# Norm statistics computed with tokens on partitions, and normalised tiles handed over one at a time

## The chip, the cores and the metric

One core of one Trainium2 chip runs the whole program. The metric is the device time of one execution in microseconds (us): lower is better.

## The reference, cut to what matters

Two layers of a transformer-like backbone over 256 tokens (128 context, 128 latent), width 2048. Each layer normalises twice, and a last norm ends the program:

```python
def rms_norm(x, g):
    y = x * rsqrt(mean(x * x, axis=-1) + 1e-6)
    return y * g

for l in range(2):
    h = rms_norm(x, g_attn[l]) * (1 + scale1) + shift1     # norm1
    x = x + gate1 * (mixers(h @ w_in[l]) @ w_out[l])       # in1, in2, in3, attention, out
    h2 = rms_norm(x, g_mlp[l]) * (1 + scale2) + shift2     # norm2
    x = x + gate2 * (square(relu(h2 @ w_mlp1[l])) @ w_mlp2[l])   # up, down
y = rms_norm(x, g_final)
```

scale, shift and gate come from a product with w_ada (the "modulation"), one vector for the context tokens and one for the latent tokens. So there are five norms: q = 0 (layer 0, norm1), 1 (layer 0, norm2), 2, 3 (layer 1) and the final one.

## The kernel before

Everything is kept transposed: `xT[128, 16, 256]` holds feature 128k + p on partition p, the 16 feature tiles k, and 256 tokens (two groups s of 128) along the row. A weight matrix streams through in "pairs": 512 columns, loaded by SyncE as four 1 MB blocks `raw`; ScalarE rounds each half block to `hi`, VectorE takes the remainder `lo = raw - hi`, and TensorE multiplies both with the activations. The activations are split too: `hs[:, k, 0:256]` is the rounded part of tile k, `hs[:, k, 256:512]` its remainder. A pair is worked in two groups g of two output banks; a group has four steps h of four tiles k each, and step h needs the half block o = 4g + h of `hi` and `lo`. A tile k costs four matmuls: 128x512 (L447) and 128x256 (L449) for each of the two banks. Between the steps, TensorE also does eight-record units of the modulation product (L388).

The order on each engine is a Python walk over stages and pairs, the same on all engines; each engine runs its queue in order, and counting semaphores tie them together. A norm stage stands before the first `in1` pair and before the first `up` pair, and goes like this:

1. TensorE: one matmul of `ones` with `ssq` (L463; L586 for the final norm) sums the squares over the partitions, and leaves the sum on every partition: a 128x256 result in bank 7.
2. ScalarE: `std` = square root of that, 128x256 (L752; final L779).
3. VectorE: `rstd` = reciprocal of `std`, 128x256 (L1019; final L1055).
4. VectorE `ybuf` = x * amul * rstd (L1024), 128x128 for each tile and token group; ScalarE adds the shift and rounds into `hs` (L759); VectorE writes the remainder (L1032). In all 32 pieces of each kind, in a hardware loop of four rounds (`Fori`, UNROLL_K = 4 tiles a round): eight L1024, then eight L1032, then a wait for the last of them.

TensorE waits before each step h for `hs_ready` to show four more finished tiles. VectorE splits o = 0, 1, 2 of the pair ahead of the norm; the split of o = 3 (`lo`, L791), which step h = 3 needs, stands behind the norm in VectorE's queue. In the final norm, VectorE writes 32 pieces `yT` (L1058) from `rstd`; TensorE turns them back and they are stored.

```python
                    own.link(dve.reciprocal(rstd[:, :], std[:, :]))
                    with dve.Fori(0, KT // UNROLL_K) as i:
                        ...
                        dve.wait_ge(hs_ready, q * NORM_STEPS + S * UNROLL_K * (i + 1))
```

Of the kernel before, what the change touches and what calls it, by code (L numbers as in the profile page):

```python
# [53 lines left out]
UNROLL_K = 4  # L54
# [42 lines left out]
def build(nc, t):  # L97
# [28 lines left out]
    ones = place("ones", [P, P], f32)  # L126
    ssq = place("ssq", [P, TOK], f32)
    std = place("std", [P, TOK], f32)
    rstd = place("rstd", [P, TOK], f32)
    cT = place("cT", [P, KT, 32], f32)  # L130
    craw = place("craw", [P, S, KT], f32)
# [53 lines left out]
    def sem(name):  # L185
        return nc.alloc_semaphore(name)
# [15 lines left out]
    relu2_ready, hid_hi = sem("relu2_ready"), sem("hid_hi")  # L202
    x_updated, sq_ready, ssq_steps = sem("x_updated"), sem("sq_ready"), sem("ssq_steps")
    stat_ready, std_ready = sem("stat_ready"), sem("std_ready")
    ada_used, rows_ready = sem("ada_used"), sem("rows_ready")
    modps_ready, mods_done = sem("modps_ready"), sem("mods_done")
    dve_step = sem("dve_step")
# [96 lines left out]
    with block:  # L304
# [71 lines left out]

        @block.tensor
        def _(pe):
            def ada_unit(l, m, a, k):

                if k == 0:
                    pe.wait_ge(rows_ready, l * VECTORS + m)
                pe.wait_ge(ada_landed[k % 2], 16 * (2 * (a - PRE_JOBS) + (k % 4) // 2 + 1))
                ada_products(k, ada[:, k % 2])
# [46 lines left out]
            for l in range(DEPTH):  # L431
                def pair(kind, n, i, c, a, last, l=l):
                    acts = act2 if kind in ("out", "down") else hs
                    for g in range(2):

                        after(pe, bank_freed, 4 * n + 2 * g - 2)
                        for h in range(4):
                            pe.wait_ge(lo_ready, 8 * n + 4 * g + h + 1)
                            if kind == "down":
                                pe.wait_ge(act2_ready, hidden_base(l, c) + 4 * (h + 1))  # L440
                            elif kind != "out":
                                pe.wait_ge(hs_ready, (2 * l + (kind == "up")) * NORM_STEPS + 8 * (h + 1))
# [140 lines left out]


            pe.wait_ge(ssq_steps, ssq_base(DEPTH, -1))
            pe.matmul(pb[7][:, 0:TOK], ones[:, :], ssq[:, :], start=True, stop=True).then_inc(stat_ready, 1)  # L586
            for b in range(8):
                s, q = b % 2, b // 2
                pe.wait_ge(yT_ready, 8 * (q + 1))
# [7 lines left out]
        def _(act):  # L597
# [33 lines left out]
            for l in range(DEPTH):  # L631
# [117 lines left out]

                def norm(q, shift, l=l):  # L750
                    act.wait_ge(stat_ready, q + 1)
                    act.activation(std[:, :], pb[7][:, 0:TOK], ACT.Sqrt, bias=eps[:, :], scale=1.0 / D)\  # L752
                       .then_inc(std_ready, 1)
                    act.wait_ge(mods_done, vectors_done(l, shift))
                    with act.Fori(0, KT // UNROLL_K) as i:
                        for k in range(UNROLL_K):
                            for s in range(S):
                                act.wait_ge(norm_y, q * NORM_STEPS + S * UNROLL_K * i + 2 * k + s + 1)
                                act.activation(hs[:, bass.ds(UNROLL_K * i + k, 1), s * P:(s + 1) * P],  # L759
                                               ybuf[:, 2 * k + s:2 * k + s + 1, :], ACT.Identity,  # L760
                                               bias=mods[:, l, bass.ds(shift + UNROLL_K * i + k, 1), s])\
                                   .then_inc(norm_hi, 1)

                def stage(name, c, l=l):
                    if name == "norm1":
# [10 lines left out]
                walk(act, l, pair, stage)  # L776

            act.wait_ge(stat_ready, 2 * DEPTH + 1)
            act.activation(std[:, :], pb[7][:, 0:TOK], ACT.Sqrt, bias=eps[:, :], scale=1.0 / D).then_inc(std_ready, 1)  # L779
# [7 lines left out]
        def _(dve):  # L787
# [38 lines left out]
            for l in range(DEPTH):  # L826
# [185 lines left out]
                def norm(q, shift, scale, gain, l=l):  # L1012
# [3 lines left out]
                        amul[:, :, :], mods[:, l, scale:scale + KT, :], 1.0,  # L1016
                        vecs[:, l, 0, gain:gain + KT].unsqueeze(2).to_broadcast([P, KT, S]), ALU.add, ALU.mult))
                    dve.wait_ge(std_ready, q + 1)
                    own.link(dve.reciprocal(rstd[:, :], std[:, :]))  # L1019
                    with dve.Fori(0, KT // UNROLL_K) as i:  # L1020
                        for k in range(UNROLL_K):
                            for s in range(S):
                                tile = bass.ds(UNROLL_K * i + k, 1)
                                dve.scalar_tensor_tensor(  # L1024
                                    ybuf[:, 2 * k + s:2 * k + s + 1, :], xT[:, tile, s * P:(s + 1) * P],
                                    amul[:, tile, s], rstd[:, s * P:(s + 1) * P].unsqueeze(1),
                                    ALU.mult, ALU.mult).then_inc(norm_y, 1)
                        for k in range(UNROLL_K):
                            for s in range(S):
                                tile = bass.ds(UNROLL_K * i + k, 1)  # L1030
                                dve.wait_ge(norm_hi, q * NORM_STEPS + S * UNROLL_K * i + 2 * k + s + 1)
                                dve.scalar_tensor_tensor(  # L1032
                                    hs[:, tile, TOK + s * P:TOK + (s + 1) * P], ybuf[:, 2 * k + s:2 * k + s + 1, :],
                                    mods[:, l, bass.ds(shift + UNROLL_K * i + k, 1), s],
                                    hs[:, tile, s * P:(s + 1) * P].bitcast(f32),
                                    ALU.add, ALU.subtract).then_inc(hs_ready, 1)
# [15 lines left out]


            dve.wait_ge(std_ready, 2 * DEPTH + 1)
            own.link(dve.reciprocal(rstd[:, :], std[:, :]))  # L1055
# [73 lines left out]
```

## Time and profile before

| what | value |
|---|---|
| median of three runs | 2477.9 us (2466.62 to 2479.76) |
| the profiled execution | 2477.66 us, span 2475.9 us |
| granted TensorE clock, mean | 0.970 |
| TensorE busy | 2307.8 us, 93% of the span |
| VectorE busy | 1535.0 us, 62% |
| ScalarE busy | 1060.9 us, 43% |
| DMA | 570.29 MB, mean 230 GB/s |

The span is from the first to the last instruction; 1.8 us of the execution lie outside it. PE in a row is TensorE's matmuls, PEld its weight loads, DVE is VectorE, ACT is ScalarE, POOL is GpSimd, and a "q" behind an engine is its sequencer. L447 is line 447 of the kernel. PEclk is the granted TensorE clock, 1.00 for 2.4 GHz and 0.50 for 1.2 GHz. A matmul on fp32 operands leaves two records; those of L447 and L449, on the split (fp32r) operands, and transposes leave one.

### The profile page before, as it was taken

To read this page: it belongs to the slowest core of one execution; us is meant where nothing else is said; L and a number is where in the kernel's file an instruction comes from. 1 tells how busy PE (TensorE), PEld (TensorE's weight loads), DVE (VectorE), ACT (ScalarE), POOL (GpSimd) and SP (SyncE) were. 2 spreads that over 40 slices of the span, in tenths; PEclk is the share of its full clock that TensorE was granted. 3 is DMA by queue.
4 is the path that set the end of the run, shared out by engine and by line. 5 is a ranking of instruction groups with operands and counts; after the bars stand their busy time and mean duration, and the time that the engine had idled before them with its cause. 6 is when DMAs were issued, how large, how long until landed. Compare 5 with 4: busy or idle time off the path is not lost.

```text
span 2475.9 us, 37816 instructions
## 1 busy us (share of the span) xinstructions
PE 2307.8 (93%) x13176; PEld 1811.7 (73%) x13176; DVE 1535.0 (62%) x2606; ACT 1060.9 (43%) x1663; POOL 101.6 (4%) x196
## 2 busy tenths in 40 slices
PE   5699879979999999999997998797999999999998
PEld 1277556757887887787785775586788888888886
DVE  0457785565665665565567578767556666666666
ACT  1243334444444444454454333444345444444443
POOL 2000000000000000000000000000000000000000
PEclk9699999989999999999998999998999999999999
DMA  9888655858678668758855885354865655655652
GB/s 387 334 311 297 232 180 208 313 206 306 207 231 305 230 203 308 267 180 295 303 170 184 297 318 208 116 177 149 314 215 181 192 182 180 193 181 192 185 189 85
DMA packets 390555, 570.29 MB, mean 230 GB/s; under 512 B 9604, under 2 KB 364472, under 8 KB 365624
## 3 DMA queue, kind: packets, MB, share of 16 engines
q1 hardware_dynamic: 360504, 365.51, 44.8%
q0 software_dynamic: 27648, 201.34, 21.5%
q10 hardware_dynamic: 2304, 2.10, 0.2%
q8 instruction: 65, 1.06, 0.2%
q14 instruction: 34, 0.28, 0.0%
HBM read 565.76 MB, written 3.15 MB: 230 GB/s over the span
## 4 chain that ended last, share of the span: by engine, by line
PE 85%; DVE 6%; DMA 4%; ACT 2%; issue 1%; DVEq 1%; POOL 0%; ACTq 0%; POOLq 0%
PE bank L447 52%; PE bank L449 26%; PE bank L388 6%; DMA ada<-in_w_ada 4%; DVE qrs L921 1%; DVE yconv L884 1%; PE bank L463 1%; DVE lo L791 1%; DVE ybuf L1024 1%; DVE hs L1032 0%; DVEq L1032 0%; ACT hs L759 0%; ACT prob L739 0%; DVE yT L1058 0%; PE bank L406 0%
## 5 line engine op out<-in xcount | busy, mean ns | idle before, releaser
L447 PE MATMUL bank<-hs,hi 128*128 128x512 f32 x2944 | 1073.8, 407 | 47.9 <-DVE hs L1032 37.2
L791 DVE TENSOR_TENSOR lo<-raw,hi 128x1024 fp32r<-128x1024 f32 x685 | 817.5, 1223 | 479.0 <-ACT hi L602 477.5
L602 ACT ACTIVATE hi<-raw 128x1024 fp32r<-128x1024 f32 x685 | 706.4, 1053 | 583.8 <-PE bank L449 580.2
L447 PE MATMUL bank<-act,hi 128*128 128x512 f32 x2560 | 910.1, 400 | 5.4 <-DVE act L972 5.4
L449 PE MATMUL bank<-hs,lo 128*128 128x256 f32 x2944 | 829.7, 282 | 0.0
L447 PEld LDWEIGHTS bank<-hs,hi 128*128 128x128 f32 x2944 | 559.7, 190 | 298.4 <-issue 143.0
L449 PE MATMUL bank<-act,lo 128*128 128x256 f32 x2560 | 720.5, 281 | 0.0
L447 PEld LDWEIGHTS bank<-act,hi 128*128 128x128 f32 x2560 | 483.1, 189 | 137.2 <-issue 13.4
L449 PEld LDWEIGHTS bank<-hs,lo 128*128 128x128 f32 x2944 | 562.2, 191 | 2.5 <-issue 2.5
L449 PEld LDWEIGHTS bank<-act,lo 128*128 128x128 f32 x2560 | 485.8, 190 | 0.0
L647 ACT ACTIVATE tmp<-bank 128x256 f32<-128x256 f32 x344 | 113.5, 382 | 394.3 <-PE bank L449 394.3
L846 DVE TENSOR_TENSOR tsum<-bank,tmp 128x256 f32<-128x256 f32 x288 | 121.4, 421 | 201.0 <-ACT tmp L647 201.0
L388 PE MATMUL bank<-ada,cT 128*32 128x512 f32 x1344 | 185.7, 626 | 8.7 <-DMA ada<-in_w_ada 8.7
L364 POOL DMA_DIRECT2D ada<-in_w_ada x160 | 84.4, 528 | 1647.6 <-PE bank L388 1631.9
L658 ACT ACTIVATE thid<-xT 128x256 f32 (+1 forms) x160 | 66.8, 418 | 156.8 <-DVE xT L855 156.8
L855 DVE SCALAR_TENSOR_TENSOR xT<-tsum,mods,xT 128x128 f32 (+1 forms) x320 | 98.3, 349 | 36.8 <-DVE tsum L846 35.6
L884 DVE SCALAR_TENSOR_TENSOR yconv<-hpad,vecs,yconv 128x256 f32<-128x256 f32 x240 | 96.7, 482 | 0.0
L871 DVE TENSOR_TENSOR ssq<-ssq,thid 128x256 f32<-128x256 f32 x160 | 67.7, 423 | 27.9 <-ACT thid L658 25.5
L652 ACT ACTIVATE act<-thid 128x256 fp32r<-128x256 f32 x128 | 53.5, 418 | 67.2 <-DVE thid L849 67.2
L388 PEld LDWEIGHTS bank<-ada,cT 128*32 128x32 f32 x1344 | 26.9, 110 | 62.1 <-issue 39.0
L863 DVE TENSOR_TENSOR act<-thid,act 128x256 fp32r<-128x256 f32 x128 | 54.0, 422 | 9.6 <-ACT act L652 3.3
L759 ACT ACTIVATE hs<-ybuf,mods 128x128 f32 x128 | 39.6, 389 | 45.5 <-DVE ybuf L1024 45.3
(127 smaller groups left out, 714.3 us busy)
## 6 DMA issues: line engine op xcount, KB each, us to landing
raw<-in_w_mlp SPq DMA_DIRECT2D x256, 1024.0 KB, 6.2
ada<-in_w_ada POOLq DMA_DIRECT2D x168, 1024.0 KB, 6.0
raw<-in_w_in SPq DMA_DIRECT2D x56, 1024.0 KB, 6.2
raw<-in_w_out SPq DMA_DIRECT2D x32, 1024.0 KB, 5.7
pre_a<-in_w_ada POOLq DMA_DIRECT2D x16, 1024.0 KB, 18.4
pre_q<-in_w_ada POOLq DMA_DIRECT2D x8, 1024.0 KB, 18.6
xtok<-in_x_prompt SPq DMA_DIRECT2D x1, 1024.0 KB, 14.2
xtok<-in_x_sample SPq DMA_DIRECT2D x1, 1024.0 KB, 32.4
```

Of the source, the lines that this page charges most:

```text
L364: pool.dma_start(ada[:, k % 2, :], src[:, k, bass.ds(m * D, D)]).then_inc(ada_landed[k % 2], 16)
L388: mm = pe.matmul(ada_ps[32 * q:32 * q + 32, :], cT[:, k, :], unit[:, q * 512:(q + 1) * 512], start=(k == 0), stop=(k == KT - 1))
L447: pe.matmul(bank[:, :], hi[:, h, k, j * P:(j + 1) * P], acts[:, k_, :], start=(k_ == 0), stop=False)
L449: mm = pe.matmul(bank[:, TOK:2 * TOK], lo[:, h, k, j * P:(j + 1) * P], acts[:, k_, 0:TOK], start=False, stop=(k_ == KT - 1))
L602: act.activation(hi[:, o % 4, :, :], raw[:, (o // 2) % 4, 4 * (o % 2):4 * (o % 2) + 4, :], ACT.Copy).then_inc(hi_ready, 1)
L647: act.activation(tmp[:, j, :], pb[2 * g + j][:, TOK:2 * TOK], ACT.Copy)\
L658: act.activation(thid[:, j:j + 1, :], xT[:, bass.ds(4 * i + 2 * g + j, 1), :], ACT.Square).then_inc(sq_ready, 1)
L791: dve.tensor_tensor(lo[:, o % 4, :, :], raw[:, (o // 2) % 4, 4 * (o % 2):4 * (o % 2) + 4, :], hi[:, o % 4, :, :].bitcast(f32), ALU.subtrac ...
L846: dve.tensor_tensor(tsum[:, j, :], bank, tmp[:, j, :], ALU.add).then_inc(bank_freed, 1)
L855: dve.scalar_tensor_tensor(x, tsum[:, j:j + 1, s * P:(s + 1) * P], mods[:, l, bass.ds(gate + 4 * i + 2 * g + j, 1), s], x, ALU.mult, ALU.a ...
L871: dve.tensor_tensor(ssq[:, :], ssq[:, :], thid[:, j, :], ALU.add)\
L884: dve.scalar_tensor_tensor(y, hpad[:, ch, :, bass.ds(tap, P)], vecs[:, l, 1, bass.ds(4 * tap + ch, 1)], y, ALU.mult, ALU.add).then_inc(con ...
```

## The change

The sums of squares are computed with the tokens on partitions: for each token group s a matmul with `ssq` as the weights and one column of ones gives a 128x1 result. Square root and reciprocal then work on 128x2. Two matmuls, with that column broadcast along the row as the weights and the identity as the moving operand, spread the reciprocals back over all partitions into the other half of bank 7; VectorE reads them from there instead of from `rstd`. The loop of four rounds becomes straight code in which tile k + 2 is scaled before tile k is finished, and in the first group of the first pair after a norm TensorE waits for each tile. The statistics of attention's convolution still use `std` and `rstd`.

```diff
+            def norm_stats(q):
+                for s in range(S):
+                    mm = pe.matmul(pb[7][:, s:s + 1], ssq[:, s * P:(s + 1) * P], ones[:, 0:1], start=True, stop=True)
+                mm.then_inc(stat_ready, 1)
+                pe.wait_ge(tok_rstd_ready, q + 1)
+                for s in range(S):
+                    mm = pe.matmul(pb[7][:, TOK + s * P:TOK + (s + 1) * P],
+                                   tok_rstd[:, s:s + 1].to_broadcast([P, P]), ident, start=True, stop=True)
+                mm.then_inc(rstd_spread, 1)
...
+                        fresh = g == 0 and isinstance(i, int) and i == 0 and (
+                            kind == "in1" or kind == "up" and isinstance(c, int) and c == 0)
...
-                            elif kind != "out":
+                            elif kind != "out" and not fresh:
                                 pe.wait_ge(hs_ready, (2 * l + (kind == "up")) * NORM_STEPS + 8 * (h + 1))
                             for k in range(4):
+                                if fresh:
+                                    pe.wait_ge(hs_ready, (2 * l + (kind == "up")) * NORM_STEPS + 8 * h + 2 * (k + 1))
...
-                        column_sums(pb[7][:, 0:TOK], [ssq[:, :]]).then_inc(stat_ready, 1)
+                        norm_stats(2 * l + (name == "norm2"))
...
-                    act.activation(std[:, :], pb[7][:, 0:TOK], ACT.Sqrt, bias=eps[:, :], scale=1.0 / D)\
+                    act.activation(tok_std[:, :], pb[7][:, 0:S], ACT.Sqrt, bias=eps[:, :], scale=1.0 / D)\
                        .then_inc(std_ready, 1)
                     act.wait_ge(mods_done, vectors_done(l, shift))
-                    with act.Fori(0, KT // UNROLL_K) as i:
...
+                    for k in range(KT):
+                        for s in range(S):
+                            act.wait_ge(norm_y, q * NORM_STEPS + S * k + s + 1)
+                            act.activation(hs[:, k, s * P:(s + 1) * P], ybuf[:, 2 * (k % UNROLL_K) + s, :], ACT.Identity,
+                                           bias=mods[:, l, shift + k, s:s + 1]).then_inc(norm_hi, 1)
...
-                    own.link(dve.reciprocal(rstd[:, :], std[:, :]))
-                    with dve.Fori(0, KT // UNROLL_K) as i:
...
+                    dve.reciprocal(tok_rstd[:, :], tok_std[:, :]).then_inc(tok_rstd_ready, 1)
+                    dve.wait_ge(rstd_spread, q + 1)
+                    for step in range(KT + 2):
+                        if UNROLL_K <= step < KT:
+                            dve.wait_ge(hs_ready, q * NORM_STEPS + S * (step - UNROLL_K + 1))
+                        if step < KT:
                             for s in range(S):
                                 dve.scalar_tensor_tensor(
+                                    ybuf[:, 2 * (step % UNROLL_K) + s, :], xT[:, step, s * P:(s + 1) * P],
+                                    amul[:, step, s:s + 1], pb[7][:, TOK + s * P:TOK + (s + 1) * P],
                                     ALU.mult, ALU.mult).then_inc(norm_y, 1)
+                        k = step - 2
+                        if k >= 0:
                             for s in range(S):
+                                dve.wait_ge(norm_hi, q * NORM_STEPS + S * k + s + 1)
                                 dve.scalar_tensor_tensor(
+                                    hs[:, k, TOK + s * P:TOK + (s + 1) * P], ybuf[:, 2 * (k % UNROLL_K) + s, :],
+                                    mods[:, l, shift + k, s:s + 1], hs[:, k, s * P:(s + 1) * P].bitcast(f32),
                                     ALU.add, ALU.subtract).then_inc(hs_ready, 1)
-                        dve.wait_ge(hs_ready, q * NORM_STEPS + S * UNROLL_K * (i + 1))
...
-                                             vecs[:, 0, 2, V_GF + k:V_GF + k + 1], rstd[:, s * P:(s + 1) * P],
+                                             vecs[:, 0, 2, V_GF + k:V_GF + k + 1], pb[7][:, TOK + s * P:TOK + (s + 1) * P],
```

The final norm takes the same statistics, `norm_stats(2 * DEPTH)` on TensorE and the 128x2 square root and reciprocal.

## Rows read from the trace of the kernel before

**Rows 1.** The page's chain that ended last: shares of the span by line.

```profile
PE bank L447 52%; PE bank L449 26%; PE bank L388 6%; DMA ada<-in_w_ada 4%; DVE qrs L921 1%; DVE yconv L884 1%; PE bank L463 1%; DVE lo L791 1%; DVE ybuf L1024 1%; DVE hs L1032 0%; DVEq L1032 0%; ACT hs L759 0%; ACT prob L739 0%; DVE yT L1058 0%; PE bank L406 0%
```

**Rows 2.** Windows (A:B, length, busy of each engine, PEclk, DMA): norms, the MLP.

```profile
102.90:125.32 22.42, 13.54 (x64) 9.53 (x64) 19.63 (x66) 11.42 (x34) 0.94 (x2) 0.72 0.44 158
498.02:523.00 24.98, 14.35 (x66) 9.78 (x66) 20.84 (x67) 12.31 (x36) 1.05 (x2) 0.73 0.14 49
506.99:511.39 4.40, 4.40 (x13) 3.73 (x14) 3.91 (x14) 2.48 (x8) 0.00 (x0) 0.50 0.00 0
525.00:1100.00 575.00, 575.00 (x3327) 459.18 (x3326) 338.53 (x512) 255.61 (x370) 24.28 (x46) 1.00 0.73 253
1319.84:1344.21 24.37, 14.38 (x66) 9.83 (x66) 20.45 (x66) 12.30 (x36) 1.05 (x2) 0.72 0.13 44
1696.68:1720.88 24.20, 14.20 (x66) 9.69 (x66) 20.23 (x66) 12.06 (x35) 1.02 (x2) 0.74 0.13 44
2459.44:2462.47 3.03, 0.70 (x2) 0.30 (x2) 1.75 (x1) 0.47 (x1) 0.00 (x0) 0.66 0.00 0
```

**Rows 3.** Waits: engine and line, what it waited for, us, times, longest.

```profile
PE bank L447 <- DVE hs L1032: 37.2, 8, 9.6
```

**Rows 4.** Timeline of the norm q = 1: start, length, engine, line.

```profile
498.02 1.22 PE L463 MATMUL bank<-ssq,ones 128*128 128x256 f32 x2 [2.68 <-DVE ssq L871]
...
501.90 2.19 DVE L1024 SCALAR_TENSOR_TENSOR ybuf<-xT,amul,rstd 128x128 f32<-128x128 f32 x8 [0.35 <-DVE rstd L1019]
504.00 2.84 DVE L1032 SCALAR_TENSOR_TENSOR hs<-ybuf,mods,hs 128x128 f32 x8
506.99 0.77 PE L447 MATMUL bank<-hs,hi 128*128 128x512 f32 x1 [7.74 <-DVE hs L1032]
507.47 2.19 DVE L1024 SCALAR_TENSOR_TENSOR ybuf<-xT,amul,rstd 128x128 f32<-128x128 f32 x8 [0.63 <-DVE hs L1032]
523.00 4.63 DVE L791 TENSOR_TENSOR lo<-raw,hi 128x1024 fp32r<-128x1024 f32 x4 [0.21 <-DVE hs L1032]
```

**Rows 5.** Timeline: eight small matmul records and a modulation unit, at both clocks.

```profile
97.39 1.88 PE L406 MATMUL bank<-cst,rows 128*128 128x8 f32 x8 [0.72 <-ACT rows L608]
...
490.46 1.07 PE L388 MATMUL bank<-ada,cT 128*32 128x512 f32 x8
...
494.39 0.95 PE L406 MATMUL bank<-cst,rows 128*128 128x8 f32 x8
```

**Rows 6.** Groups by line and form: busy us, mean ns, idle before.

```profile
L602 ACT ACTIVATE hi<-raw 128x1024 fp32r<-128x1024 f32 x685 | 706.4, 1053 | 583.8 <-PE bank L449 580.2 <-issue 0.7
...
L1001 DVE RECIPROCAL rinv<-rsum 128x2 f32<-128x2 f32 x24 | 3.9, 164 | 1.7 <-ACT prob L739 1.2
...
L742 ACT ACTIVATE esink<-nb,sinks 128x2 f32<-128x2 f32 x12 | 3.5, 290 | 0.0
```

**Rows 7.** Timeline in attention: one 128x128 product (two records) at both clocks.

```profile
348.18 0.63 PE L566 MATMUL bank<-probT,vtok 128*128 128x128 f32 x2
...
354.43 0.39 PE L544 MATMUL bank<-kcT,zq 128*128 128x128 f32 x2
```

**Rows 8.** Timeline of the final norm: 32 pieces in straight code.

```profile
2462.47 8.49 DVE L1058 SCALAR_TENSOR_TENSOR yT<-xT,vecs,rstd 128x128 f32<-128x128 f32 x32
```

**Rows 9.** VectorE's sequencer at L1032: count, min/median/max ns.

```profile
L1032 DVEq FUSED_REGOPS  x224: 65/93/99, 106.6 to 1720.2; - x112
```

**Rows 10.** Groups: VectorE with a PSUM operand, without one, without and with a pointer operand.

```profile
L846 DVE TENSOR_TENSOR tsum<-bank,tmp 128x256 f32<-128x256 f32 x288 | 121.4, 421 | 201.0 <-ACT tmp L647 201.0
L884 DVE SCALAR_TENSOR_TENSOR yconv<-hpad,vecs,yconv 128x256 f32<-128x256 f32 x240 | 96.7, 482 | 0.0
...
L871 DVE TENSOR_TENSOR ssq<-ssq,thid 128x256 f32<-128x256 f32 x160 | 67.7, 423 | 27.9 <-ACT thid L658 25.5
L849 DVE SCALAR_TENSOR_TENSOR thid<-tsum 128x256 f32<-128x256 f32 x128 | 54.5, 425 | 4.4
```

**Rows 11.** A window in attention, TensorE alone: length, busy, PEclk, DMA.

```profile
366.00:368.00 2.00, 1.09 (x8) 1.00 0.05 21
```

More of the change, by code:

```diff
@@ L128, in build @@
     std = place("std", [P, TOK], f32)
+    tok_std = place("tok_std", [P, S], f32)
+    tok_rstd = place("tok_rstd", [P, S], f32)
     rstd = place("rstd", [P, TOK], f32)
@@ L204, in build @@
     stat_ready, std_ready = sem("stat_ready"), sem("std_ready")
+    tok_rstd_ready, rstd_spread = sem("tok_rstd_ready"), sem("rstd_spread")
     ada_used, rows_ready = sem("ada_used"), sem("rows_ready")
@@ L585, in _ @@
             pe.wait_ge(ssq_steps, ssq_base(DEPTH, -1))
-            pe.matmul(pb[7][:, 0:TOK], ones[:, :], ssq[:, :], start=True, stop=True).then_inc(stat_ready, 1)
+            norm_stats(2 * DEPTH)
             for b in range(8):
@@ L751, in norm @@
                     act.wait_ge(stat_ready, q + 1)
-                    act.activation(std[:, :], pb[7][:, 0:TOK], ACT.Sqrt, bias=eps[:, :], scale=1.0 / D)\
+                    act.activation(tok_std[:, :], pb[7][:, 0:S], ACT.Sqrt, bias=eps[:, :], scale=1.0 / D)\
                        .then_inc(std_ready, 1)
                     act.wait_ge(mods_done, vectors_done(l, shift))
-                    with act.Fori(0, KT // UNROLL_K) as i:
[L756 to L762, printed above, removed]
+                    for k in range(KT):
[3 more added lines that the diff above has]
+                                           bias=mods[:, l, shift + k, s:s + 1]).then_inc(norm_hi, 1)
                 def stage(name, c, l=l):
@@ L778, in _ @@
             act.wait_ge(stat_ready, 2 * DEPTH + 1)
-            act.activation(std[:, :], pb[7][:, 0:TOK], ACT.Sqrt, bias=eps[:, :], scale=1.0 / D).then_inc(std_ready, 1)
+            act.activation(tok_std[:, :], pb[7][:, 0:S], ACT.Sqrt, bias=eps[:, :], scale=1.0 / D).then_inc(std_ready, 1)
             for b in range(8):
@@ L1018, in norm @@
                     dve.wait_ge(std_ready, q + 1)
-                    own.link(dve.reciprocal(rstd[:, :], std[:, :]))
-                    with dve.Fori(0, KT // UNROLL_K) as i:
-                        for k in range(UNROLL_K):
+                    dve.reciprocal(tok_rstd[:, :], tok_std[:, :]).then_inc(tok_rstd_ready, 1)
[4 more added lines that the diff above has]
+                        if step < KT:
@@ L1022, in norm @@
                             for s in range(S):
-                                tile = bass.ds(UNROLL_K * i + k, 1)
                                 dve.scalar_tensor_tensor(
-                                    ybuf[:, 2 * k + s:2 * k + s + 1, :], xT[:, tile, s * P:(s + 1) * P],
-                                    amul[:, tile, s], rstd[:, s * P:(s + 1) * P].unsqueeze(1),
+                                    ybuf[:, 2 * (step % UNROLL_K) + s, :], xT[:, step, s * P:(s + 1) * P],
+                                    amul[:, step, s:s + 1], pb[7][:, TOK + s * P:TOK + (s + 1) * P],
@@ L1027, in norm @@
                                     ALU.mult, ALU.mult).then_inc(norm_y, 1)
-                        for k in range(UNROLL_K):
+                        k = step - 2
+                        if k >= 0:
                             for s in range(S):
-                                tile = bass.ds(UNROLL_K * i + k, 1)
-                                dve.wait_ge(norm_hi, q * NORM_STEPS + S * UNROLL_K * i + 2 * k + s + 1)
+                                dve.wait_ge(norm_hi, q * NORM_STEPS + S * k + s + 1)
@@ L1032, in norm @@
                                 dve.scalar_tensor_tensor(
-                                    hs[:, tile, TOK + s * P:TOK + (s + 1) * P], ybuf[:, 2 * k + s:2 * k + s + 1, :],
-                                    mods[:, l, bass.ds(shift + UNROLL_K * i + k, 1), s],
-                                    hs[:, tile, s * P:(s + 1) * P].bitcast(f32),
+                                    hs[:, k, TOK + s * P:TOK + (s + 1) * P], ybuf[:, 2 * (k % UNROLL_K) + s, :],
+                                    mods[:, l, shift + k, s:s + 1], hs[:, k, s * P:(s + 1) * P].bitcast(f32),
@@ L1054, in _ @@
             dve.wait_ge(std_ready, 2 * DEPTH + 1)
-            own.link(dve.reciprocal(rstd[:, :], std[:, :]))
+            dve.reciprocal(tok_rstd[:, :], tok_std[:, :]).then_inc(tok_rstd_ready, 1)
+            dve.wait_ge(rstd_spread, 2 * DEPTH + 1)
             for k in range(KT):
```

## The prediction

> **What bounds the kernel now.** I read the chain that ended last first: 78% of the span is the two matmul lines L447 and L449, and every line of the norm has 1% or less [rows 1]. In the MLP stretch TensorE is busy for all of 575.00 us at clock 1.00 [rows 2]. So only stretches in which TensorE stands still can give anything. The waits name the one that this change touches: L447 waited 37.2 us for L1032, in eight waits [rows 3], four at the starts of the norms q = 0 to 3 and four inside them. The windows, cut from the moment at which the norm's own chain can begin (in q = 0 the end of the splits ahead of the reciprocal, else the matmul of ones) to the start of the `lo` split for step h = 3, show 22.42, 24.98, 24.37 and 24.20 us, with TensorE busy 13.5 to 14.4 us of each; the final norm needs 3.03 us from matmul to first piece [rows 2].
>
> The timeline of q = 1 says what fills such a window [rows 4]. 498.02 to 501.90, 3.88 us: matmul of ones at the low clock (1.22), square root, reciprocal, start of the loop (0.35 idle). 501.90 to 523.00, 21.1 us: four rounds of eight L1024 in 2.19 us and eight L1032 in 2.84 us, with 0.63 us idle between rounds. TensorE starts at 506.99. But that start does not set the end of the stage: step h = 3 needs `lo` of o = 3, which begins behind the last L1032 at 523.00 and takes 1.2 us of the 4.63. VectorE's chain through the norm is the bound, and whatever shortens it moves the rest of the program, which is solid TensorE work, by as much. An earlier first matmul alone gives nothing.
>
> **The change, part by part.** *Statistics.* New: two one-column matmuls. The nearest rows are four products with eight columns in 0.95 us at the high clock and 1.88 us at the low one [rows 5], so 0.48 or 0.94 us for two. A ScalarE operation on 128x2 takes 0.29, a reciprocal on 128x2 0.16 [rows 6], where the 128x256 one took 1.75 (DVE busy in the window of the final norm [rows 2]). Spreading: two 128x128 products, each 0.63 us at the low clock and 0.39 at the high [rows 7], 1.26 or 0.78 us if they don't overlap (the lower bound is one of them, 0.39). Four hand-overs between engines: the final norm's 3.03 us hold 0.70, 0.47 and 1.75 us of work and so 0.11 us for three [rows 2], 0.04 each, 0.15 to 0.2 us. Sum: 0.94 + 0.29 + 0.16 + 1.26 + 0.2 = 2.8 us at the low clock; 2.4 us if the first pair still runs high, which I take for q = 2; 1.9 us for the final norm, all high. In q = 0 the statistics lie under VectorE's three splits already, and only reciprocal, spreading and hand-overs stay: 1.5 us. TensorE's new wait for the reciprocal delays nothing: behind it are only the matmuls that need the norm. No DMA is moved, and SyncE's and POOL's queues keep their order.
>
> *The tiles.* VectorE still issues 64 pieces of 128x128. In straight code 32 of them took 8.49 us [rows 8], which is (8.49 - 0.35) / 31 = 0.263 us from start to start. L1024 holds that pace in the loop, (2.19 - 0.35) / 7 = 0.263; L1032 takes up to (2.84 - 0.35) / 7 = 0.356 [rows 4], and its sequencer spent 224 register operations of 93 ns on 128 pieces [rows 9]. Straight code has constants there and none of the pauses between rounds. Bounds for one L1032: 0.263 and 0.356; I take 0.263, since the only thing the loop adds goes. Then piece 64 ends 63 x 0.263 + 0.35 = 16.9 us after the first starts. ScalarE, behind piece 58 (15.3 us), needs 0.4 for its last tile and 1.05 for `hi` of o = 3 [rows 6]: 16.8. So the `lo` split starts at 17.2, with 0.2 to 0.3 us of gap as before.
>
> *PSUM operand.* L1024 and L1058 now read bank 7. A 128x256 operation with a PSUM operand took 421 ns, one without 423; what does cost is a pointer operand, 482 against 425 [rows 10], and those pieces have it already. I take 0; the bounds are 0 and the 57 ns of that pair, 160 pieces x 0.057 = 9.1 us. The Trainium skill speaks against this edit: VectorE: DVE Perf Modes, section "The TRN2 errata", gives VectorE a fixed 58 cycles from SBUF and 120 from PSUM; as an estimate that is 65 ns x 160 = 10.3 us, so about 2469 instead of 2459. Both rows at 421 to 423 ns speak against it.
>
> *Hand-over by tile.* Tile k is whole after piece 4k + 8: tile 0 at 2.2 us, tile 11 at 51 x 0.263 + 0.35 = 13.8 us. A tile's four matmuls take 0.69 us at the high clock (575 us for 3327 records) and 0.63 x 2 = 1.26 at the low (seven pairs in 4.40 us [rows 2]). TensorE follows the tiles and is through with h = 2 and two modulation units of 1.07 us [rows 5] at about 13.8 + 0.7 + 1.3 = 15.8 us, before the first `lo` is there at 17.2 + 1.2 = 18.4. This edit is worth nothing by itself: what hides it is the wait for `lo`; without that cover it would be worth up to 2.6 us a stage.
>
> **The sum.** Stages after: 1.5 + 17.2 = 18.7; 2.8 + 17.2 = 20.0; 2.4 + 17.2 = 19.6; 20.0. Against [rows 2]: 3.7 + 5.0 + 4.8 + 4.2, and 3.0 - 1.9 = 1.1 for the final norm: 18.8 us. The profiled execution took 2477.66 us, within 0.3 of the median: 2477.7 - 18.8 = 2459 us, 0.76% faster.
>
> **Rivals.**
> *PSUM reads cost.* 57 ns on each of 160 pieces: 2468. For it, no row; against it [rows 10].
> *The pieces keep their pace.* If the 0.356 us of L1032 comes from its wait on ScalarE and not from the registers, 32 x 0.093 = 3.0 us a stage come back, 12 us: 2471. For it: L1032 is the line with a wait. Against: ScalarE is two tiles ahead now.
> *The low clock holds.* Handing over by tile leaves TensorE busy 0.69 of each 1.05 us, 66%, for 12 us. If the clock stayed at 1.2 GHz, twelve tiles take 15.1 us and two units 4.3: ready at 2.2 + 19.4 = 21.6, 3.2 later than `lo`, and step h = 3 costs 2.3 more: 5.5 x 4 = 22 us, 2481. Against it: in attention TensorE was busy 1.09 of 2.00 us at clock 1.00 [rows 11]. The Trainium skill (TensorE: Matmul & The Clock Gate, "A second HAM failure mode: psum-queue depth-cycling") has a kernel in which short idle times between groups made the clock swing; that is this rival.
> *Slower than before.* The same mechanism carried on: 18.8 + 12.4 = 31 us must be lost, so the low clock must also last through another step and a half of full TensorE work in every stage (2.3 us for each step): about 2492. Against it: in q = 1 TensorE, once fed, spent only 4.40 us at 0.50 [rows 2].
>
> **How the numbers follow.** A measurement here can tell about 0.5% from no change, 12.4 us: 2465.5 is the border. Forecast, 2450 to 2465, 0.70; below 2450 (the lowest run of before lay 11 us under its median) 0.06; PSUM 0.09; pace 0.07; low clock 0.05; slower 0.03. Range 2450 to 2470: it takes in the PSUM bound and, nearly, the pace rival; 0.80 or a little more lies inside. Faster: 0.70 + 0.06 + 0.02 of the PSUM case that falls short of its bound = 0.78; same 0.19; slower 0.03.
>
> **What the profile after would show.** Right: from first to last piece of a norm about 17 us, L1024 and L1032 interleaved at 0.263; small reciprocal 0.16 us; L447's first wait for L1032 shorter by about 4 us, and the wait for `lo` before h = 3 left at 2 to 3 us; the window up to that split 19 to 20 us; the MLP stretch unchanged. Wrong: pieces from bank 7 longer than 350 ns; PEclk 0.50 beyond the first 6 us of tiles; TensorE still at h = 2 when `lo` is there.

## The result, and the profile after

The changed kernel takes 2440.57 us (median of 4 runs, 2439.11 to 2461.4) where the kernel before, in the same session, takes 2477.69 (4 runs, 2466.62 to 2479.76): ratio 0.9876, 95% interval 0.9841 to 0.991. That is 37 us faster, twice the 18.8 us of the sum and below the range of 2450 to 2470. The profiled execution took 2439.11 us (span 2437.4), 38.55 us less than the profiled one before.

The chain of the page answers [rows 1]: the same two matmul lines (now L466 and L468), with the same shares.

```profile
PE bank L466 52%; PE bank L468 26%; PE bank L403 6%; DMA ada<-in_w_ada 4%; DVE hs L1050 1%; DVE ybuf L1042 1%; DVE qrs L937 1%; DVE yconv L900 1%; DVE lo L807 1%; PE bank L482 0%; ACT prob L758 0%; DVE yT L1075 0%; PE bank L421 0%; PE bank L390 0%; PE bank L510 0%
```

Windows of the changed kernel. Those of q = 1, q = 2, q = 3 and the final norm are cut at the same events as in [rows 2]. Then come TensorE's first tiles of q = 1 in two windows, from its first matmul at 500.49 to 505.00 and on to 509.40, and the MLP stretch.

```profile
495.35:514.86 19.51, 15.51 (x72) 11.21 (x72) 17.09 (x68) 12.18 (x35) 0.87 (x2) 0.75 0.18 61
1303.25:1322.35 19.10, 15.47 (x72) 11.01 (x72) 16.91 (x67) 12.18 (x35) 0.58 (x2) 0.73 0.17 56
1677.34:1696.85 19.51, 15.43 (x72) 10.84 (x72) 16.89 (x66) 12.18 (x35) 0.89 (x2) 0.77 0.15 54
2421.97:2424.12 2.15, 1.56 (x8) 1.18 (x8) 0.17 (x1) 0.26 (x1) 0.00 (x0) 0.85 0.00 0
500.49:505.00 4.51, 4.51 (x14) 3.83 (x15) 4.51 (x19) 2.97 (x9) 0.00 (x0) 0.50 0.00 0
505.00:509.40 4.40, 4.40 (x28) 2.97 (x27) 4.40 (x19) 3.01 (x10) 0.53 (x1) 0.98 0.18 32
525.00:1100.00 575.00, 575.00 (x3364) 462.04 (x3363) 341.09 (x515) 257.63 (x373) 23.77 (x45) 1.00 0.74 254
```

The four stages came out a little shorter than forecast: 19.51, 19.10 and 19.51 us against 20.0, 19.6 and 20.0; q = 0, from the reciprocal at 103.09 to the split at 121.24, 18.15 against 18.7. The final norm is a little longer than forecast, 2.15 us against 1.9. Against [rows 2] they give 4.27 + 5.47 + 5.27 + 4.69 + 0.88 = 20.6 us. Some 18 us of the 38.5 between the two spans are not in the norms.

The timeline of q = 1 (start, length, engine, line) shows the new chain: 2.83 us from 495.35 to 498.18, the first tile of TensorE 2.31 us after the first piece, and the last pieces running into the split of step h = 3.

```profile
495.35 1.01 PE L386 MATMUL bank<-ones,ssq 128*128 128x1 f32 x4 [2.68 <-DVE ssq L887]
496.41 0.26 ACT L771 ACTIVATE tok_std<-bank,eps 128x2 f32<-128x2 f32 x1 [1.56 <-PE bank L386]
496.70 0.17 DVE L1035 RECIPROCAL tok_rstd<-tok_std 128x2 f32<-128x2 f32 x1 [1.07 <-ACT tok_std L771]
496.92 1.22 PE L390 MATMUL bank<-cst,tok_rstd 128*128 128x128 f32 x4 [0.55 <-DVE tok_rstd L1035]
498.18 1.64 DVE L1042 SCALAR_TENSOR_TENSOR ybuf<-xT,amul,bank 128x128 f32<-128x128 f32 x6 [1.31 <-PE bank L390]
...
500.49 0.76 PE L466 MATMUL bank<-hs,hi 128*128 128x512 f32 x1 [2.35 <-DVE hs L1050]
...
513.28 1.66 DVE L1050 SCALAR_TENSOR_TENSOR hs<-ybuf,mods,hs 128x128 fp32r<-128x128 f32 x6
514.86 1.22 DVE L807 TENSOR_TENSOR lo<-raw,hi 128x1024 fp32r<-128x1024 f32 x1
```

The waits that answer [rows 3]: 37.2 us on the norm's tiles have become 9.4, and TensorE's new wait for the small reciprocal is 4.7. The wait for `lo` was there before and is nearly what it was, 10.7 and now 9.6 us. First a line of the kernel before, then three of the changed one:

```profile
PE bank L447 <- DVE lo L791: 10.7, 6, 2.6
```

```profile
PE bank L466 <- DVE lo L807: 9.6, 6, 2.3
PE bank L466 <- DVE hs L1050: 9.4, 4, 2.4
PE bank L390 <- DVE tok_rstd L1035: 4.7, 4, 3.0
```

**Where the other 18 us are.** The group of L666 (`tmp`, the first read of each finished bank) gives the moments at which groups of matmuls end. Here it is for the MLP of layer 1, 57 groups with no modulation unit among them, of the kernel before (L647) and then of the changed one (L666); the last numbers are the first and the last start:

```profile
L647 ACT ACTIVATE tmp<-bank x114: 378/383/385, 1821.9 to 2456.3; 128x256 f32<-128x256 f32 x114
```

```profile
L666 ACT ACTIVATE tmp<-bank x114: 378/382/385, 1796.4 to 2418.8; 128x256 f32<-128x256 f32 x114
```

634.4 us against 622.4: 12.0 us less in a stretch in which nothing was edited. Both kernels show TensorE 100% busy at clock 1.00 there, so the windows cannot see it. The groups by form can. Line L447 or L466 in layer 0's first `down` stretch (640 to 700) and in layer 1's MLP (1900 to 2400), kernel before:

```profile
L447 PE MATMUL bank<-act,hi 128*128 128x512 f32 x171 | 60.5, 399 | 0.0
...
L447 PE MATMUL bank<-act,hi 128*128 128x512 f32 x649 | 229.5, 399 | 0.0
```

and the changed kernel:

```profile
L466 PE MATMUL bank<-act,hi 128*128 128x512 f32 x175 | 60.7, 394 | 0.0
...
L466 PE MATMUL bank<-act,hi 128*128 128x512 f32 x716 | 248.3, 394 | 0.0
```

A tile step, one 512-column and one 256-column product, starts every 0.3533 us in the one and every 0.3467 us in the other (means over the start times). I call these the long and the short pace. Layer 0's four `down` stretches of 264 steps come to 4 x 264 x 0.0067 = 7.0 us, layer 1's MLP of 1792 steps to 11.9: 18.9 us, which with the 20.6 of the stages makes up the 38.5 within a microsecond (layer 1's attention took 1.1 us more).

Both paces are in every profile. Through the stretches with modulation units they alternate: a burst of 16 steps at the short pace, a unit, a burst at the long one. Over the 14 profiles of this case the pace changed at 1923 of the 1986 units that stand between two bursts. In the kernels without extra units, a stretch without units keeps the pace of the last burst ahead of it to its end, up to 630 us later. Which pace that is therefore hangs on where the few exceptions fall. So what was to be tested was whether this pace is the change's doing.

### The profile page after: what moved, and what is told of

It is laid out like the page before. It is cut to its first block, busy times and chain, and to the rows that moved or that the text cites. A ratio compares the mean times of both kernels' runs of the same rounds, so it can differ in the third digit from the quotient of the medians.

```text
span 2437.4 us, 36896 instructions
## 1 busy us (share of the span) xinstructions
PE 2293.2 (94%) x13206; PEld 1808.6 (74%) x13206; DVE 1520.0 (62%) x2606; ACT 1060.4 (44%) x1663; POOL 101.6 (4%) x196
## 3 DMA queue, kind: packets, MB, share of 16 engines
q0 software_dynamic: 27648, 201.34, 21.9%
q8 instruction: 65, 1.06, 0.2%
HBM read 565.76 MB, written 3.15 MB: 233 GB/s over the span
## 4 chain that ended last, share of the span: by engine, by line
PE 86%; DVE 7%; DMA 4%; ACT 2%; issue 1%; POOL 0%; ACTq 0%; DVEq 0%; POOLq 0%
PE bank L466 52%; PE bank L468 26%; PE bank L403 6%; DMA ada<-in_w_ada 4%; DVE hs L1050 1%; DVE ybuf L1042 1%; DVE qrs L937 1%; DVE yconv L900 1%; DVE lo L807 1%; PE bank L482 0%; ACT prob L758 0%; DVE yT L1075 0%; PE bank L421 0%; PE bank L390 0%; PE bank L510 0%
## 5 line engine op out<-in xcount | busy, mean ns | idle before, releaser
L466 PE MATMUL bank<-hs,hi 128*128 128x512 f32 x2944 | 1068.4, 406 | 19.2 <-DVE lo L807 9.6
L466 PE MATMUL bank<-act,hi 128*128 128x512 f32 x2560 | 895.6, 396 | 5.4 <-DVE act L988 5.4
L468 PE MATMUL bank<-hs,lo 128*128 128x256 f32 x2944 | 826.6, 281 | 0.0
L466 PEld LDWEIGHTS bank<-hs,hi 128*128 128x128 f32 x2944 | 559.5, 190 | 265.9 <-issue 112.9
L468 PE MATMUL bank<-act,lo 128*128 128x256 f32 x2560 | 712.1, 278 | 0.0
L466 PEld LDWEIGHTS bank<-act,hi 128*128 128x128 f32 x2560 | 481.7, 188 | 129.9 <-issue 13.4
L468 PEld LDWEIGHTS bank<-hs,lo 128*128 128x128 f32 x2944 | 561.3, 191 | 2.5 <-issue 2.5
L468 PEld LDWEIGHTS bank<-act,lo 128*128 128x128 f32 x2560 | 483.1, 189 | 0.0
L666 ACT ACTIVATE tmp<-bank 128x256 f32<-128x256 f32 x344 | 113.3, 382 | 384.7 <-PE bank L468 384.7
L865 DVE SCALAR_TENSOR_TENSOR thid<-tsum 128x256 f32<-128x256 f32 x128 | 54.4, 425 | 4.4
## 6 DMA issues: line engine op xcount, KB each, us to landing
pre_a<-in_w_ada POOLq DMA_DIRECT2D x16, 1024.0 KB, 18.8
pre_q<-in_w_ada POOLq DMA_DIRECT2D x8, 1024.0 KB, 18.8
```

What stands on the lines that cost most here:

```text
L666: act.activation(tmp[:, j, :], pb[2 * g + j][:, TOK:2 * TOK], ACT.Copy)\
```

## The experiments

**The changed kernel once more** (no edit).

> The changed kernel once more, beside the kernel before. Two theories. Theory A: the change shortens the four norm stages and the final norm, by about 20 us in all; the other 18 us of the first comparison are a pace of TensorE in the groups of matmuls that hold no modulation unit, 11.09 us a group against 11.31, which is picked in each execution and can fall to either kernel. Then the times of each kernel lie in clusters: the changed one near 2440 and near 2461, the one before near 2478, near 2466 and, if both layers come out fast, near 2458. Theory B (rival): the new order of the norm fixes the fast pace: all runs of the changed kernel within 2 us of 2440, none near 2461, and the one before never below 2466.

2438.06, 2440.38, 2440.47, 2445.88, 2451.52, 2458.93: ratio 0.9869 (0.9837 to 0.9902). The profiled run, 2445.88 us, has every stage as above (2.83 and 2.41 us to the first piece, 16.67 and 16.68 from there to the split), the long pace in layer 0 and the short one in layer 1:

```profile
L466 PE MATMUL bank<-act,hi 128*128 128x512 f32 x171 | 60.5, 399 | 0.0
...
L466 PE MATMUL bank<-act,hi 128*128 128x512 f32 x696 | 241.4, 394 | 0.0
```

2445.88 - 2439.11 = 6.8 us, the 7.0 of layer 0's stretches. The pace is not fixed by the program: it differs between runs of one kernel, so theory B is out, and the gain is 37 us with some luck in it. The final norm depends on the granted clock: 2.07 us here, 2.15 in the first profile, and 2.83 in other profiles of the changed kernel.

**The statistics alone** (loop and waits of before, spread statistics). The cut shows the edit against the changed kernel.

```
                     dve.wait_ge(rstd_spread, q + 1)
-                    for step in range(KT + 2):
+                    with dve.Fori(0, KT // UNROLL_K) as i:
...
+                                    amul[:, tile, s], pb[7][:, TOK + s * P:TOK + (s + 1) * P].unsqueeze(1),
...
-                        fresh = g == 0 and isinstance(i, int) and i == 0 and (
+                        fresh = False
```

> Only the statistics are changed; the loop of four rounds, with its pauses and the waits for four tiles, is kept. By the terms of the prediction: from the matmul of the sums to the first scaled piece 2.8 us where it was 3.9, from there to the split of o = 3 unchanged at 20.3 to 21.1 us, in sum 5 us less than before: 2473 at the slow pace of TensorE, 2452 to 2455 at the fast one. Theory B, if the statistics are what sets the pace: all runs near 2453.

Median 2476.91 of ten (2459.73 to 2481.53), ratio 0.9986 (0.9963 to 1.0009). The way to the first piece is 3.15 us where it was 3.88 (q = 1), the rest of the stage stays at 20.3 to 21.1:

```profile
499.46:523.71 24.25, 15.54 (x72) 11.34 (x72) 19.21 (x68) 12.09 (x36) 1.06 (x2) 0.73 0.15 52
```

Up to 0.7 us a stage and 0.6 to 1.1 in the final norm, under 4 us in all, is less than this measurement can tell. The expectation had 5 us, with 2.8 us to the first piece: of the 3.15, 0.36 lie idle between the spreading and the first piece, as 0.35 did in the loop of before [rows 4], and only the straight code drops them.

**The straight code and the waits by tile alone** (statistics of before, so all operands in SBUF). The cut shows the edit against the kernel before.

```
                     own.link(dve.reciprocal(rstd[:, :], std[:, :]))
-                    with dve.Fori(0, KT // UNROLL_K) as i:
+                    for step in range(KT + 2):
...
+                                    amul[:, step, s:s + 1], rstd[:, s * P:(s + 1) * P],
...
+                                if fresh:
+                                    pe.wait_ge(hs_ready, (2 * l + (kind == "up")) * NORM_STEPS + 8 * h + 2 * (k + 1))
```

> Only the straight order of the tiles and TensorE's wait for each tile; square root and reciprocal stay on 128x256. By the terms of the prediction: 3.5 to 3.9 us to the first piece as before, then 17.2 us to the split of o = 3 instead of 20.3 to 21.1, in sum 14 us less: 2464 at the slow pace, 2443 at the fast one. Theory B, if the order of the tiles sets the pace: all runs near 2443.

2455.78 us (2444.25 to 2464.75), ratio 0.9915 (0.9886 to 0.9945). First piece to split: 16.82 us in all four stages, 20.3 to 21.1 before, so 3.5 to 4.3 us each. The window of q = 1, and the piece that reads SBUF here:

```profile
494.80:515.17 20.37, 14.45 (x66) 9.30 (x66) 18.80 (x67) 12.40 (x35) 0.90 (x2) 0.78 0.17 59
...
L1026 DVE SCALAR_TENSOR_TENSOR ybuf<-xT,amul,rstd 128x128 f32<-128x128 f32 x128 | 38.2, 344 | 0.1
L1034 DVE SCALAR_TENSOR_TENSOR hs<-ybuf,mods,hs 128x128 fp32r<-128x128 f32 x128 | 38.2, 343 | 0.0
```

The same lines of the changed kernel, in which `ybuf` (L1042) reads bank 7:

```profile
L1050 DVE SCALAR_TENSOR_TENSOR hs<-ybuf,mods,hs 128x128 fp32r<-128x128 f32 x128 | 38.4, 347 | 0.0
L1042 DVE SCALAR_TENSOR_TENSOR ybuf<-xT,amul,bank 128x128 f32<-128x128 f32 x128 | 37.9, 343 | 5.3 <-PE bank L390 5.3
```

344 ns from SBUF, 343 from PSUM, and 16.82 against 16.68 us from first piece to split: the PSUM operand costs nothing.

**The changed kernel without the waits by tile.**

```
- fresh = g == 0 and isinstance(i, int) and i == 0 and (...)
+ fresh = False
```

> The changed kernel without TensorE's wait for each tile: it waits for four tiles again. The split of o = 3 should still be what step h = 3 waits for, so the same time as the changed kernel at the same pace, within 1 us (2440 or 2461). Rival: the early start of TensorE is worth something, for instance by bringing its clock up sooner: 2 us or more slower than the changed kernel at the same pace.

2442.9 us (2438.42 to 2450.45), ratio 0.9866 (0.9834 to 0.9898), the same as with them. TensorE's first tile starts 5.44 us after the first piece instead of 2.31, and the wait for `lo` has moved to the tiles:

```profile
PE bank L465 <- DVE hs L1049: 21.9, 4, 5.5
...
PE bank L465 <- DVE lo L806: 0.7, 2, 0.3
```

So the cover was just used up. The first `tmp` behind the split of h = 3 comes 21.1 us after the first piece in q = 0 and q = 1, as with the waits by tile, but 21.6 and 21.9 us after it in q = 2 and q = 3.

**One extra modulation unit ahead of the first `down` stretch of each layer**, in the kernel before and in the changed one, to turn the pace over.

```
+ elif name == "clear" and isinstance(c, int) and c == 0:
+     for q in range(4):
+         pe.matmul(pb[6][32 * q:32 * q + 32, :], cT[:, 0, :], cst[:, 0:512], start=True, stop=True)
```

> The kernel before with four more 32x512 products of the modulation's shape, on constants, into an unused bank, once in each layer between the last up pair of the first chunk and its down pairs (added work, 1.2 us each; its result is not used). In six profiles the pace of the matmul steps changes between 0.3467 and 0.3533 us with every modulation unit, and a stretch without units keeps the pace of the last steps ahead of it. If each unit turns the pace over, the first down stretch here has the other pace than the steps before the extra unit, in both layers, and the times move with it: the kernel before, mostly slow in both layers (2478 to 2484), comes out mostly near 2461 to 2465. Rival: the pace of the long stretches hangs on something else (the code of the loop, the data): then down stays at 0.3533 and the time is 2480 to 2486.

> The changed kernel with the same extra units. If each unit turns the pace over: the changed kernel, mostly fast in both layers (2438 to 2441), now mostly 2459 to 2463, and its own gain over the kernel with the extra units and the old norm stays near 20 us at the same pace. Rival: the change itself makes the long stretches fast: 2441 to 2444.

Before with the unit: 2484.33 us, all twelve runs from 2483.73 to 2488.18, ratio 1.0037 (1.0022 to 1.0052). After with it: 2459.5, six runs from 2458.81 to 2462.61, ratio 0.9937 (0.9916 to 0.9958). The spread is gone, and both stand at the long pace in their profiles. For the changed kernel that was expected. For the kernel before 2461 to 2465 was, and the time came out where the rival had put it, though nothing here shows the rival's reasons, the code of the loop or the data. TensorE's timeline in the changed kernel with the unit shows the place: a burst at the short pace, the eight small records of L421 (they stand there without an extra unit too, and the pace stays the same across them), the unit (L602, 1.06 us), and L466 at the long pace behind it:

```profile
612.65 0.39 PE L466 MATMUL bank<-hs,hi 128*128 128x512 f32 x1
612.88 0.27 PE L468 MATMUL bank<-hs,lo 128*128 128x256 f32 x1
612.99 0.40 PE L466 MATMUL bank<-hs,hi 128*128 128x512 f32 x1
613.22 0.28 PE L468 MATMUL bank<-hs,lo 128*128 128x256 f32 x1
613.34 0.95 PE L421 MATMUL bank<-cst,rows 128*128 128x8 f32 x8
614.22 1.06 PE L602 MATMUL bank<-cst,cT 128*32 128x512 f32 x8
615.22 0.50 PE L466 MATMUL bank<-act,hi 128*128 128x512 f32 x1
...
615.68 0.39 PE L466 MATMUL bank<-act,hi 128*128 128x512 f32 x1
...
616.03 0.40 PE L466 MATMUL bank<-act,hi 128*128 128x512 f32 x1
```

This makes the comparison that the first pair of profiles does not allow, the change at one pace: 2484.33 - 2459.5 = 24.8 us. The two profiles (spans 2482.2 and 2458.6, 23.6 apart) account for it. Norm windows, from the same events: 22.40 + 24.97 + 24.83 + 23.69 + 3.56 = 99.45 us against 18.16 + 19.51 + 19.51 + 19.50 + 2.83 = 79.51, 19.9 less. From the split of h = 3 to the first `tmp` behind it: 23.28 us in the four stages against 17.63, 5.7 less. Layer 1's `out` stretch had the short pace in the one and the long one in the other, 1.7 us back. 19.9 + 5.7 - 1.7 = 23.9.

The 5.7 us are the clock. Windows from that split to `tmp`, the changed kernel in q = 0 and q = 1, then the same kernel with the unit in q = 0:

```profile
121.24:127.17 5.93, 4.65 (x17) 4.03 (x18) 4.63 (x5) 2.77 (x3) 0.19 (x1) 0.71 0.78 257
514.86:519.22 4.36, 3.08 (x17) 2.73 (x18) 4.36 (x5) 2.77 (x4) 0.18 (x1) 1.00 0.71 249
```

```profile
121.28:125.68 4.40, 3.13 (x17) 2.75 (x18) 4.40 (x5) 2.77 (x3) 0.17 (x1) 1.00 0.79 246
```

TensorE waits there for `lo`, and in some stages its granted clock falls from 1.00 (2.4 GHz) to the low level (1.2 GHz) once more, which costs 1.5 us. In the first pair of profiles both kernels paid this twice. It was 17 of 20 stages with the norm's loop of before (five profiles) and 7 of 20 in the changed kernel (its own two profiles and three with extra units). The straight code with the old statistics paid it in three stages of four, so the count is no plain property of the straight code. It goes with the wait: in these 44 stages TensorE stood still for 2.0 to 2.6 us ahead of the split's first product, and each fall began in that wait or up to 1.3 us behind it. In the 12 stages of the three profiles in which TensorE's waits for `lo` are at most 0.3 us (without the waits by tile, and the split taken into the norm, below) the clock never fell. Why it falls behind some of these waits and not behind others is open.

**The split of h = 3 taken into the norm**, the step that the windows point to: TensorE waits for `lo`, and VectorE has all it needs for it earlier. ScalarE's `hi` split of the same step goes ahead of its part of the norm.

```
                     for step in range(KT + 2):
+                        if step == 12:
+                            split_lo(l * PAIRS_LAYER + (IN1 + IN2 + IN3 + OUT if q % 2 else 0), 3)
```

> The changed kernel with the split of o = 3 moved: ScalarE rounds it ahead of its square root, VectorE takes the remainder in the middle of the tiles, at step 12, so that step h = 3 doesn't wait behind the norm. If that wait is the bound of the stage, as the prediction says, TensorE starts step h = 3 about 2 us sooner in each of the four norms: 8 us less at the same pace, 2430 to 2433 where both layers are fast and 2450 to 2453 where both are slow. Rival: TensorE is the bound itself by then, and the 1.2 us of the split delay the last tiles: within 2 us of the changed kernel at the same pace.

2444.78 us (2432.16 to 2452.68), ratio 0.9866 (0.9834 to 0.9897). Windows from the split to the first `tmp`, q = 0 and q = 1:

```profile
116.18:124.52 8.34, 7.04 (x39) 4.70 (x38) 8.34 (x24) 5.67 (x13) 0.53 (x1) 1.00 0.66 222
507.07:515.41 8.34, 7.36 (x42) 5.05 (x41) 8.34 (x24) 5.66 (x13) 0.53 (x1) 1.00 0.80 258
```

`tmp` now comes 11.46 + 8.34 = 19.8 us after the first piece in every stage, where it was 21.1 or, with the fall of the clock, 22.6; that fall is gone. Four stages give 5 to 11 us. The profiled run, 2444.1 us, had the long pace in layer 1's MLP; less 11.9 that is 2432.2, and two of the six runs stand there, 2432.16 and 2433.7, where the changed kernel's lowest is 2438.06. The medians cannot tell the two apart (2444.78 and 2443.18): the pace spreads them by more than the edit gives.

**The kernel before once more** (no edit), profiled once.

> The kernel before, for one more profile. Norm stages as in the first profile to 0.1 us (3.9, 3.4 and 3.9 us to the first piece, 20.3 to 21.1 from there to the split); the pace of the down stretches one of 0.3467 and 0.3533 us in each layer, constant through each layer's MLP. If the pace is picked once per stretch with even chances, fast in both layers would show in one of four.

2483.35 us, long pace in all three stretches and four falls of the clock. The ways to the first piece are 3.87, 3.86 and 3.35 us, where 3.9, 3.4 and 3.9 were expected. With the first profile: 2483.35 - 2477.66 = 5.7 us, against 1.7 (`out`) + 2 x 1.5 = 4.7 counted.

**Two extra units, and one in layer 1 alone**, to see whether a unit turns the pace over or sets it. Kernel before and changed kernel with two (the loop runs over `range(8)`), changed kernel with `and l == 1`, and the split-inside kernel with two.

> The kernel before, with two extra modulation units (eight matmuls 32x512, results unused) instead of one ahead of the first down stretch of each layer. Two units should cost about 2 x 1.1 x 2 = 4.4 us at most by themselves. Theory A (each unit turns the pace of the two-matmul step over, 0.3467 to 0.3533 us and back, and the pace ahead of the unit was the short one in every profile with one extra unit): with two units the down stretches of both layers run at 0.3467, about 18.7 us less than with one unit: 2484.3 - 18.7 + 2.2 = 2468 us, and steady within 3 us. Theory B (an extra unit there always leaves the long pace behind, whatever was before): 2484.3 + 2.2 = 2486.5, steady. Theory C (the steadiness with one unit was chance): times spread over 2465 to 2487 as those of the kernel before do.

> The changed kernel with the same two extra units. Theory A: 2459.5 - 18.7 + 2.2 = 2443 us, steady within 3 us, and 25 us below the kernel before with two units, as with one (24.8). Theory B: 2461.7, steady. Theory C: spread from 2442 to 2463.

> The changed kernel with one extra unit in layer 1 alone. If what the unit does is bound to its own place, the layer 1 MLP stretch runs at 0.3533 in every run (11.9 us more than the all-fast 2438.5, so none below 2450) and the layer 0 stretch at either pace, as in the changed kernel: values near 2451.5 and near 2458.5. If the extra unit acts on the whole program (by where the instructions lie), layer 0 is slow in every run too: all near 2458.5.

> The changed kernel with the split of step h = 3 taken into the norm, and two extra units. Theory A: the all-fast value of that kernel, about 2432, + 4.4 for the two pairs of units = 2436 us, steady. Theory B: 2432 + 20.6 + 4.4 = 2457, steady. Theory C: spread from 2436 to 2457.

Before with two: 2477.49 (2467.4 to 2490.12, ten runs), ratio 0.9996 (0.9974 to 1.0019). After with two: 2466.06 (2452.79 to 2467.98, five), ratio 0.9932 (0.9904 to 0.996). After with one in layer 1: 2457.39 (2455.29 to 2458.45, four), ratio 0.9911 (0.9887 to 0.9935). Split inside with two: 2445.18 (2443.4 to 2447.63, four), ratio 0.9867 (0.9842 to 0.9891). With two units the spread is back, which neither A nor B would have. A also rested on a reading that was not right: in the kernel before with one unit, layer 0's last burst ahead of the unit had the long pace. In the three profiles with two units the first stretch behind them had the pace of the burst ahead of them: long after long four times, short after short twice. Behind one unit it was long in all five cases of the three profiles, four times after a short burst and once after a long one. The times with two units hold something else as well: in both such profiles of the changed form (the second with the split inside) TensorE stands idle twice for 2.8 to 3.5 us, at the ends of the second and third `down` stretch of layer 0, 5.7 and 6.3 us in all. None of the other twelve profiles has an idle time of TensorE there. The cause is not known. So these two kernels are no clean test of the pace by their times.

Layer 1's unit kept every run above 2450, as expected, but those runs also stand where layer 0's long pace would put them, more often than its own spread suggests. And one layer can hold both paces; the changed kernel with two units, first `down` stretch and third:

```profile
L466 PE MATMUL bank<-act,hi 128*128 128x512 f32 x171 | 60.5, 399 | 0.0
...
L466 PE MATMUL bank<-act,hi 128*128 128x512 f32 x174 | 60.4, 394 | 0.0
```

## Why the prediction was wrong

**The stages, right.** They were to give 18.8 us and gave 20.6. The sum's terms, as measured: statistics 2.83 us (forecast 2.8) and 2.42 (2.4), final norm 2.15 (1.9), q = 0 from reciprocal to first piece 1.48 (1.5); first piece to split 16.68 (17.2), since the 63 steps ran at 0.26 us and ScalarE's last tiles left no gap ahead of the split. "The pieces keep their pace" fell by that. The experiments do not separate the registers from the order of the tiles, which changed with them, but the trace of before does:

```profile
502.48 2.68 ACT L759 ACTIVATE hs<-ybuf,mods 128x128 f32 x8 [2.73 <-DVE ybuf L1024]
504.00 2.84 DVE L1032 SCALAR_TENSOR_TENSOR hs<-ybuf,mods,hs 128x128 f32 x8
```

ScalarE is through with its eight pieces at 505.16, and all 128 pieces of L1032 begin 1.0 to 1.4 us after ScalarE's part of the same piece has ended. So no wait on ScalarE made the 0.356 us; what is left is the loop's own work on VectorE's sequencer [rows 9].

**The PSUM operand at 0, right.** 343 ns against 344. The estimate of 65 ns more from the Trainium skill (VectorE: DVE Perf Modes, "The TRN2 errata") disagrees with these rows, which decide.

**Hand-over by tile worth nothing by itself, right in the time.** 2442.9 us without it, 2443.18 and 2440.57 with it; what it saves at the tiles is waited for at `lo`. The cover was thinner than the prediction had it: without the hand-over the first `tmp` came 0.5 and 0.8 us later in two stages (in none of the four did the clock fall).

**The low clock would not hold, right.** In q = 1 it was 0.50 for the first 4.51 us of tiles and 0.98 from 505.00 on; the rival's 2481 and 2492 us did not come. But the clock can fall a second time behind the stage, which the prediction did not have: on average (17 - 7) / 20 x 4 x 1.5 = 3 us for the change, and 5.7 in the pair with the unit.

**The step that failed** is "whatever shortens it moves the rest of the program, which is solid TensorE work, by as much", and with it "the MLP stretch unchanged". Solid work is not work of a fixed length: its steps take 0.3467 or 0.3533 us, layer 0's and layer 1's long stretches each hold one pace, and between all short and all long lie 7.0 + 1.7 + 11.9 = 20.6 us, a little more than the forecast gain. The profile before had the long pace in both layers, the one after the short pace in both. Taken back to the pace of before, the profiled execution would be 2439.11 + 7.0 + 11.9 = 2458.0, where 2459.0 was forecast; and with the unit, at the long pace throughout, 2459.5 was measured. The range took its width from the costs of the edits alone and had no term for this, though both signs were there: [rows 2] gives 575.00 us busy, which says nothing of the pace, but the start times inside that window alternate between the two, and the runs of before spread over 13 us. The prediction had seen that spread and gave a time below 2450 a chance of 0.06, but did not ask what makes it.

**What is shown and what is open.** Shown: the change by itself is worth 24.8 us at the long pace, 1.0%, and in the first two profiles the pace makes up 18.9 of the 38.5 us. That the rest of the 37, some 12 us, is the changed kernel's runs having the short pace more often is read from their times, since a run shows its pace only in a profile, and there are two of each kernel. Of the changed kernel's ten runs seven lie between 2438 and 2446; of 55 runs of the kernel before none is below 2466.59, while the short pace in both layers would put it near 2459 (2477.66 - 18.9). So the kernel before hardly ever had both, and the changed one often. Straight code alone shows both too (2444.25 to 2464.75), with the statistics alone one run of ten is at 2459.73 and the next at 2467.55. Why is open. The profiles of the changed kernel differ in it from the first bursts behind a norm stage on, and it is handed on from burst to burst; but nothing tried here sets it to short, and one unit, two units and their place gave no rule that holds for all. Whether the norm's end time, the clock's rise or the place of the instructions picks it was not separated.

## What to carry to other kernels

Before a stretch is called solid, look at the start times or the mean length of its commonest instruction, not at the busy share: 399 and 394 ns at 100% busy and clock 1.00 were worth 19 us here. When the gain of an edit is found outside the stretch that was edited, compare the two kernels with that other quantity held equal (here by one small dummy unit that fixed it), and quote both numbers, what the edit gives and what the runs give. In a stage bound by one engine's chain, ask what makes its last product late: here it was the loop, 3.5 to 4.3 us a stage, and then the split that stood behind the pieces though it could run between them.

## What the runs showed of the hardware

- TensorE at granted clock 1.00 runs one and the same sequence (512 and 256 columns) at two paces, 0.3533 and 0.3467 us a step, and keeps one for 1792 steps. After a modulation unit (1.07 us, other shapes) it changed in 1923 of 1986 cases; one extra unit ahead of the long stretch made all 18 runs of two kernels agree within 4.5 us each, at the long pace.
- The granted clock can fall to the low level in a wait of TensorE of 2.0 to 2.6 us, or up to 1.3 us behind it; it did so in 7 of 20 and 17 of 20 stages, at 1.5 us each, and in none of the 12 stages without that wait.
- A VectorE piece of 128x128 with a pointer operand takes 343 ns with its third operand in PSUM and 344 with it in SBUF.
